# A decoder layer on eight cores: norm statistics in column halves, three chunks at a time; attention in 26 steps; 16-column back products; a last feed-forward group in parts

## What is computed

```python
h = x * (1 + sc1) + sh1                          # adaLN, from c
q, k, v, pool_in, ga, gb = split(h @ w_in)
# branch A: 3 groups (window, dilation) of 4 heads, banded 128-blocks, ALiBi, softmax;
#           the groups of a head slot are mixed by their softmax denominators
branch_a = att @ w_branch_att
# branch B: trailing means over 2/4/8/16 positions minus the token, per-group linear map
branch_b = (pooled @ w_pool_group * pool_scale) @ w_branch_pool
mixer_out = (sigmoid(ga) * branch_a + sigmoid(gb) * branch_b) @ w_out
x = layer_norm(alpha * x + g1 * mixer_out)
h2 = x * (1 + sc2) + sh2
ffn = (silu(h2 @ w_gate) * (h2 @ w_up)) @ w_down
x = layer_norm(alpha * x + g2 * ffn)             # D_MODEL 1024, SEQ 2048, D_FF 2816
```

## Time and profile before

| what | value |
|---|---|
| time, median of 3 runs | 2016.94 us (2016.87 to 2017.34) |
| the profiled execution | 2017.5 us, span of the slowest core 2016.1 us |
| span of the eight cores | 2013.8 to 2016.1 us, mean granted TensorE clock 0.995 |
| TensorE busy | 1941.8 us, 96% of the span |
| VectorE, ScalarE, GpSimd busy | 891.0, 781.1, 139.8 us |
| TensorE in the chain that ended last | 95% |

### The profile page before, as it was taken

How to read it: one execution, slowest core, us unless ns; L and a number is a source line. 1 busy time by engine, 2 the same in 40 slices (tenths; PEclk the granted TensorE clock), 3 DMA queues, 4 the chain that set the end, 5 groups by cost and what they waited for, 6 DMA issues and landing times.

```text
span 2016.1 us, 33562 instructions; the slowest of 8 cores (2013.8 to 2016.1 us)
## 1 busy us (share of the span) xinstructions
PE 1941.8 (96%) x11808; PEld 998.1 (50%) x11808; DVE 891.0 (44%) x1417; ACT 781.1 (39%) x1343; POOL 139.8 (7%) x268
## 2 busy tenths in 40 slices
PE   1999999999999999999999999999999999999995
PEld 0566654444446544444455566444444664444442
DVE  0446643552326435525265664354232553552326
ACT  0555532641026326410266553255101632651026
POOL 1110100000000000100000000000000000000000
PEclk9999999999999999999999999999999999999998
DMA  9965843444345635557451125344444473444432
GB/s 193 229 96 101 149 123 63 74 79 78 67 81 126 157 63 115 84 115 158 73 121 38 33 54 133 68 74 64 74 83 77 102 189 64 74 71 72 77 64 84
DMA packets 58962, 193.49 MB, mean 96 GB/s; under 512 B 6832, under 2 KB 6832, under 8 KB 57520
## 3 DMA queue, kind: packets, MB, share of 16 engines
q0 software_dynamic: 38016, 136.20, 40.7%
q1 hardware_dynamic: 20784, 55.14, 8.5%
HBM read 300.24 MB, written 18.87 MB: 158 GB/s over the span
## 4 chain that ended last, share of the span: by engine, by line
PE 95%; DMA 2%; DVE 1%; ACT 1%; issue 1%; POOL 0%; DVEq 0%; ACTq 0%; SPq 0%; POOLq 0%
PE ps L372 84%; PE ps L1024 4%; PE ps L805 3%; PE ps L621 2%; PE ps L594 1%; DMA T<-xT 1%; DMA wring<-w_ada 1%; DVE T L832 1%; DVE T L838 0%; PE ps L415 0%; DVE T L939 0%; ACT sg_t L985 0%; ACT u_t L507 0%; ACT hT L468 0%; POOL wring L189 0%
## 5 line engine op out<-in xcount | busy, mean ns | idle before, releaser
L372 PE MATMUL ps<-T,wring 128*128 128x512 bf16 x4864 | 1078.5, 379 | 4.2 <-ACT sg_t L985 4.2
L372 PEld LDWEIGHTS ps<-T,wring 128*128 128x128 bf16 x4864 | 475.7, 98 | 578.9 <-issue 6.7
L372 PE MATMUL ps<-hT,wring 128*128 128x512 bf16 x1792 | 413.9, 381 | 13.8 <-ACT hT L468 13.4
L985 ACT ACTIVATE sg_t<-ps 128x512 f32<-128x512 f32 x176 | 103.2, 596 | 553.3 <-PE ps L372 546.5
L986 DVE TENSOR_TENSOR T<-ps,sg_t 128x512 bf16<-128x512 f32 x176 | 120.2, 691 | 421.1 <-PE ps L372 379.7
L939 DVE SCALAR_TENSOR_TENSOR T<-ps,GA,T 128x512 f32<-128x512 f32 x256 | 192.1, 750 | 208.5 <-PE ps L372 206.4
L372 PEld LDWEIGHTS ps<-hT,wring 128*128 128x128 bf16 x1792 | 170.0, 98 | 219.2 <-issue 26.8
L372 PE MATMUL ps<-wring,hT 128*128 128x256 bf16 x1856 | 214.3, 273 | 2.1 <-ACT u_t L507 1.7
L372 PEld LDWEIGHTS ps<-wring,hT 128*128 128x128 bf16 x1856 | 184.3, 107 | 23.8 <-issue 2.9
L608 DVE TENSOR_TENSOR T<-ps,bias_t 128x256 f32<-128x256 f32 (+1 forms) x232 | 107.0, 499 | 61.7 <-PE ps L594 47.1
L613 ACT ACTIVATE T<-T 128x256 bf16<-128x256 f32 (+1 forms) x232 | 104.0, 478 | 69.8 <-DVE T L608 63.1
(11 more groups left out here) (80 smaller groups left out, 1072.0 us busy)
## 6 DMA issues: line engine op xcount, KB each, us to landing
wring<-w_gate POOLq DMA_DIRECT2D x44, 512.0 KB, 6.6
wring<-w_up POOLq DMA_DIRECT2D x44, 512.0 KB, 7.0
T<-xT SPq DMA_DIRECT2D x32, 512.0 KB, 9.5
wring<-w_down POOLq DMA_DIRECT2D x32, 512.0 KB, 7.2
outT<-T SPq DMA_DIRECT2D x64, 256.0 KB, 4.3
T<-xT SPq DMA_DIRECT2D x14, 1024.0 KB, 11.3
wring<-w_ada POOLq DMA_DIRECT2D x24, 512.0 KB, 8.8
wring<-w_pi POOLq DMA_DIRECT2D x16, 512.0 KB, 6.2
```

What stands on the lines that cost most here:

```text
L372: fns = [lambda lhsT=lhsT, rhs=rhs, i=i: nc.tensor.matmul(psum[bank][:, cols[0]:cols[1]], lhsT, rhs, start=(i == 0), stop=(i == n - 1)) fo ...
L985: k.op(ACT, lambda: nc.scalar.activation(sg_t[:, si, :], psum[bg][:, :], AF.Silu), reads=[ps_reg[bg]], writes=[r_sg[si]])
```

## The change

1. **Norm statistics.** The stationary matrix is now 128x64. The product with the copy goes to partitions 0 to 63 and that with the square to partitions 64 to 127 of one held bank, by the left and the right column half of the array. They are issued for three chunks in one group, when four chunks are fed: with chunk n fed, chunks n-3 to n-1. The staging has six buffers (three more lie in `t12_t`). Mean and mean square now stand on half of the partitions each, so `ln_moments` has three ScalarE operations in place of two and `ln_rstd` three in place of two.
2. **Attention.** `att_all` replaces the six phases by 26 steps over all of them. A step issues the outs of two block pairs (those scored two steps earlier), the scores of two block pairs, and then the other units, with the bias and exp operations between them. There are eight softmax buffers for each head of the pair instead of six. Units of the pooling branch (`pj[2]`, `bd[1]`, `pj[3]`) that stood behind attention are spread over the last six steps.
3. **Bands.** The back product has 16 columns instead of 128, and a unit is one group.
4. **The end.** In the last half of the last sequence the weights of the last gate and up products are loaded into `hT`, which is free by then, and the group is computed by token half: gate, up and down products of tt=0; gate and up of tt=1 with the norm passes of tt=0 between them; and down products of tt=1 in two quarters of 256 columns, each with its own statistics and norm.
5. Norm passes of the second norm are split in two background steps each.

```diff
--- before
+++ after
-LAG = 2
-NPT = 6
+NPT = 8
...
-        def att_phase(ph, fill, vroll):
-            scores, out = att_parts(ph)
-            n = 8 + LAG
-            share = spread(fill, n)
-            for i in range(n):
-                if i < 8:
-                    scores(i)
-                for f in share[i]:
-                    f()
-                if i >= LAG:
-                    o = i - LAG
-                    out(o)
-                    if o >= 1 and vroll:
-                        vroll[o - 1]()
-            if vroll:
-                vroll[7]()
+        def att_all(fills):
+            parts = [att_parts(ph) for ph in range(6)]
+            vnext = {ph: v_units(ph // 2 + 1, ACT) for ph in (1, 3)}
+            for t in range(26):
+                fill = list(fills[t])
+                if t >= 2:
+                    po, so = divmod(t - 2, 4)
+                    for pr in (2 * so, 2 * so + 1):
+                        parts[po][1](pr)
+                    if po in vnext:
+                        ready = 8 if so == 3 else 2 * so + 1
+                        vu = vnext[po]
+                        fill += vu[:ready - (8 - len(vu))]
+                        del vu[:ready - (8 - len(vu))]
+                post = []
+                if t < 24:
+                    ph, sp = divmod(t, 4)
+                    for pr in (2 * sp, 2 * sp + 1):
+                        post += parts[ph][0](pr)
+                n = max(len(fill), 1)
+                for i in range(max(n, len(post))):
+                    if i < len(post):
+                        post[i]()
+                    if i < len(fill):
+                        fill[i]()
...
+                            opening = hf == 0 and tau == 1
+                            mm(s_ * 128, 128, tau, 2 if opening else 0, True, opening)
+                            if not opening:
+                                mm(s_ * 128, 16, tau - 1, 1, False, True)
...
-            i0 = 2 * (feed["n"] % 3)
...
+            i0 = feed["n"] % 6
             feed["n"] += 1
-            k.op(ACT, lambda: nc.scalar.copy(ybs_t[:, i0, :], ysrc), reads=yreg, writes=[r_ybs[i0]])
-            k.op(ACT, lambda: nc.scalar.activation(ybs_t[:, i0 + 1, :], ysrc, AF.Square), reads=yreg, writes=[r_ybs[i0 + 1]])
-            feed["q"].append((key, m, i0))
-            while len(feed["q"]) > 2:
-                stats_pe()
-
-        def stats_pe():
-            key, m, i0 = feed["q"].pop(0)
-            if m == 0:
-                stat[key] = (new_bank(hold=True), new_bank(hold=True))
-            for j in range(2):
-                bk = stat[key][j]
-                k.group([lambda bk=bk, j=j: nc.tensor.matmul(psum[bk][:, :], onesm[:], ybs_t[:, i0 + j, :], start=(m == 0), stop=(m == KC - 1))],
-                        reads=[r_ybs[i0 + j], r_ones], writes=[ps_reg[bk]])
+            k.op(ACT, lambda: nc.scalar.copy(stat_buf(i0, 0, w), ysrc), reads=yreg, writes=stat_regs(i0))
+            k.op(ACT, lambda: nc.scalar.activation(stat_buf(i0, 1, w), ysrc, AF.Square), reads=yreg, writes=stat_regs(i0))
+            feed["q"].append((key, m, i0, w))
+            if len(feed["q"]) > 3:
+                stats_pe(3)
...
+        def stats_pe(n):
+            fns, rds, wrs = [], [r_ones], []
+            for _ in range(n):
+                key, m, i0, w = feed["q"].pop(0)
+                if m == 0:
+                    stat[key] = new_bank(hold=True)
+                bk = stat[key]
+                for j in range(2):
+                    fns.append(lambda bk=bk, j=j, m=m, i0=i0, w=w: nc.tensor.matmul(
+                        psum[bk][64 * j:64 * j + 64, 0:w], onesm[:, 0:64], stat_buf(i0, j, w), start=(m == 0), stop=(m == KC - 1)))
+                rds += stat_regs(i0)
+                wrs.append(ps_reg[bk])
+            k.group(fns, reads=rds, writes=wrs)
...
+        def ln_moments(key, si, w=512):
+            bk = stat[key]
+            s1 = 2 + 2 * si
+            mean = psum[bk][0:64, 0:w]
+            k.op(ACT, lambda: nc.scalar.activation(st_t[64:128, 0, 0:w], mean, AF.Square), reads=[ps_reg[bk]], writes=[r_st[0]])
+            k.op(ACT, lambda: nc.scalar.copy(st_t[0:64, s1, 0:w], mean), reads=[ps_reg[bk]], writes=[r_st[s1]])
+            k.op(ACT, lambda: nc.scalar.copy(st_t[64:128, s1, 0:w], mean), reads=[ps_reg[bk]], writes=[r_st[s1]])
+
+        def ln_rstd(key, si, w=512):
+            bk = stat[key]
+            s0 = 1 + 2 * si
+            var = st_t[64:128, 0, 0:w]
+            k.op(DVE, lambda: nc.vector.tensor_tensor(var, psum[bk][64:128, 0:w], var, ALU.subtract),
+                 reads=[ps_reg[bk], r_st[0]], writes=[r_st[0]])
...
+            for p0 in (0, 64):
+                k.op(ACT, lambda p0=p0: nc.scalar.activation(st_t[p0:p0 + 64, s0, 0:w], var, AF.Exp, scale=-0.5), reads=[r_st[0]], writes=[r_st[s0]])
...
+        def closing_loads(f0):
+            def mk(q, src):
+                return lambda: k.dma(POOL, tl_h[q], [(hT[:, q, :].rearrange("p (k c) -> p k c", c=256), src)], writes=r_hT[q])
+            return [mk(q, src[f0 // 2 + i]) for i in range(4) for q, src in ((i, w_gate), (4 + i, w_up))]
...
+            run([f1_unit(b, f0, fl, 0, st) for fl in range(nf)], bg, 1)
+            while bg:
+                bg.pop(0)()
+            for m in range(KC):
+                if m % 2 == 0:
+                    slots[m // 2] = wload(down_load(f0, f1, m // 2))
+                f2_unit(b, nf, m, 0, slots, False)()
+                stats_feed((b, 2, 0), m, 0, 512)
+            units = [f1_unit(b, f0, fl, 1, st) for fl in range(nf)]
+            units[0]()
+            stats_flush()
+            ln_moments((b, 2, 0), 0)
+            units[1]()
+            ln_rstd((b, 2, 0), 0)
+            bg = ln2_steps(b, t0, 0, 512, 0)
+            run(units[2:], bg, 2)
+            for q in range(2):
+                c0 = 512 + 256 * q
+                for m in range(KC):
+                    f2_unit(b, nf, m, c0, slots, False, 256)()
+                    stats_feed((b, 2, 1 + q), m, c0, 256)
+                    if q == 0:
+                        if bg:
+                            bg.pop(0)()
+                    else:
+                        if m == 1:
+                            ln_moments((b, 2, 1), 1, 256)
+                        elif m == 2:
+                            ln_rstd((b, 2, 1), 1, 256)
+                            bg = ln2_steps(b, t0, 512, 256, 1)
+                        elif m > 2:
+                            bg.pop(0)()
+                            bg.pop(0)()
+            stats_flush()
+            ln_moments((b, 2, 2), 0, 256)
+            ln_rstd((b, 2, 2), 0, 256)
+            return bg + ln2_steps(b, t0, 768, 256, 0)
...
+            last = spread(pj[0] + pj[1] + bd[0] + pj[2] + bd[1] + pj[3], 6)
+            for i in range(4):
+                last[2 + i] = last[2 + i] + nu[2 * i:2 * i + 2]
+            att_all(fills + last)
...
-            run(pj[2] + bd[1] + pj[3] + bd[2] + bd[3], bg, 1)
+            run(bd[2] + bd[3], bg, 1)
```

213 lines of the change are left out of this document (107 added, 106 removed).

## The result

| kernel | time, median | ratio to before |
|---|---|---|
| before | 2017.1 us | 1 |
| after | 2060.1 us (2060.44 and 2059.68) | 1.0213, 95% interval 1.0191 to 1.0235 |

The change makes the kernel 2.1% slower (1.9 to 2.4%). In two of the four runs of after (2352.7 and 2420.7 us) one die ran at a lower granted clock, 0.81 to 0.85 against 0.985 of the other die; they are left out. The forecast was 2022 us with a range to 2036: the sign was right, and the time lies 24 us above the range and 38 us above the forecast. All comparisons with before that follow are ratios on the same chip; the median of before was 2017 to 2023 us on the chips used.

What follows compares the result with a forecast made beforehand. TensorE, busy 96% of the span, was taken as the bound; -17.3 + 3.5 - 7.2 - 2.4 + 30.4 - 2.0 = +5.0 us on the median of 2016.94 gives 2022 us. Own range 2013 to 2031, full range 2006 to 2036.

Steps and rivals of the forecast that it cites:

- The clock rival: TensorE's clock falls in each of seven 3.6 us statistics waits: +18 us, 2040 us; chance 0.10.
- n = 12 waits: Statistics group at n = 12 waits for chunk 11's square behind ScalarE's moments and 1/sigma: 3.6 us a norm.
- Statistics: Norm statistics in column halves, one unit behind: waits of 7.1 us a norm outweigh saved products, +30.4 us for seven norms.
- the rival of 2048 us: Column halves of the statistics products do not run together at 512 columns: +26 us, 2048 us; chance 0.03.
- form changes: Switches of the TensorE array's form between neighbouring matmuls, in attention and statistics: 0.10 us each.
- Attention: New attention order has 148 changes of array form instead of 321: -17.3 us, with new waits counted against it.
- +3.5 us of waits: New TensorE waits in attention, at t=23's scores (2.4 us for two sequences) and phase boundaries (about 1.1); bounds 0 and 6.
- Bands: In the band units, 240 back products of 16 columns save 0.030 us each: -7.2 us, bounds 0 and -7.7.
- The part -2.4 for u_t: Pooling units' waits for u_t go because the norm's VectorE passes are spread over twice the units: -2.4 us.
- The end: Last group by token half with a half-size closing chain: 111.8 against 113.8 us, -2.0 us, bounds -6 and +3.
- The sum: All terms over the whole kernel: +5.0 us, giving 2022 us; chance of the forecast 0.45.

Runs made afterwards that it cites:

- fill mixed: Changed kernel with statistics and end of before, and projection and band units of the last six attention steps reordered; ratio to before 0.9900, 2003 us.

## Why the prediction was wrong, point by point

**The clock rival had the right size and the wrong chance.** This is the step that failed: the sum put the clock behind the new waits at nothing, and it is 23 of the 38 us by which the forecast was missed. The rival asked for 2.6 us behind each of seven 3.6-us waits, +18 us, and got a chance of 0.10 with the reason that the trace of before has no wait of such a length behind the start. But the earlier trace rows were a case of exactly this mechanism, with nothing that speaks against it at 3.6 us (the windows of the profile print a clock of 1.00 there only because the trace has no clock record ahead of 53.80 us; half speed from 48.51 to 53.80 is a loss of 2.6 us, the figure that the rows give); the forecast itself created seven waits in which it could act, and then left the price out of the sum. In the profile of after the seven n = 12 waits carry 30.7 us of half clock, 13.9 us of time; filling them gave back 12.3 us. So even the rival's +18 was somewhat high for these seven; attention (5.5 us) and the closing group (3.8) make it 23 us. What the Trainium skill says in "TensorE: Matmul & The Clock Gate", Part 1, that an idle stretch puts the clock back to its lower level, agrees with these rows. What no row of before could tell is that the clock would also fall behind the attention waits of 1.2 and 2.0 us, whose ends are 2.4 us apart.

**Statistics: right.** Forecast +30.4 for seven norms without the clock, thus 34.7 for eight. The kernel with the statistics alone has eight: +53 us, less 17 us of clock, is +36. The waits were forecast as 0.85, 0.85, 0.85, 3.6 and 1.0, and are 0.77, 0.77, 0.70, 3.81 and 0.70 to 1.08. The n = 12 chain came out as counted: moments, cast, square, table load, exp, exp, cast and square of chunk 11 in a row on ScalarE.

```profile
379.61 0.59 ACT L853 ACTIVATE st_t<-ps 64x512 f32<-64x512 f32 x1
...
382.92 1.28 ACT L863 ACT_TABLE_LOAD   x1
...
385.02 1.34 ACT L866 ACTIVATE st_t<-st_t 64x512 f32<-64x512 f32 x2
386.39 0.62 ACT L825 CAST t_t<-T 128x512 bf16<-128x512 f32 x1
387.10 0.63 ACT L826 ACTIVATE t_t<-T 128x512 bf16<-128x512 f32 x1
```

Square now starts 0.71 behind cast instead of 0.52; that both write one buffer with one entry in the register of hazards, so that the second waits for the first, is the reading of the code and was not tried. It is small beside the rest. Column halves at 512 columns do run together, six in 0.77 us: the rival of 2048 us did not come. The rule of the Trainium skill beside it ("TensorE: Matmul & The Clock Gate", Part 3, The mechanism: a weight load overlaps only across row groups) does not hold for these groups by the same 0.77 us. A group without a wait adds 0.875 - 0.648 = 0.23 us of form changes where I had 0.20. A misreading without effect on the sum: the largest waits of before behind the start are not those for u_t but four of up to 1.0 us for L985, 4.2 us in all.

**Attention: the saving right, the waits too small.** -17.5 against -17.3 for the forms. This is the second term that was mis-sized: the sum had +3.5 us of waits in all, and in the two attention stretches of after TensorE waits 8.2 and 4.8 us, where before it waited 0 and 0.8, so +12.2. The place was named (t = 22, its scores at t = 23) and priced 1.2 us per sequence; there it is 4.4 us, since L739 waits for L656 twice, the out products wait for the adds 1.22 and the scores 2.01; and each time the clock falls. Attention was to be some 14 us shorter in two sequences, and the two stretches are 3.0 us shorter. The working set VectorE's work of the step (5.9 us) against TensorE's (3.6) and took the lag at one point only, the scores. In after it shows at four points that add up, 0.37 + 0.77 + 1.22 + 2.01 = 4.4 us.

**Bands: products right, the sum too good.** 0.025 us per short product against 0.026. The bands alone gave 4.5 us of the 7.2, because 2.0 us of new waits for u_t stand against them. The part -2.4 for u_t was laid to the norm passes, and in the kernels that have them about 1 us of these waits is left.

**The end: -2.0 forecast, +3.0 measured** against the end of before, with old statistics; in after it is +8.4 us. I had put 1.2 us in front of each of the two changes from gate and up to down; the first is 1.2, the second 5.25. The cause is seen in the timeline of VectorE and ScalarE there:

```profile
1990.37 0.69 DVE L1026 TENSOR_TENSOR T<-ps,sg_t 128x512 bf16<-128x512 f32 x1 [3.42 <-PE ps L377]
...
1995.33 1.28 ACT L1025 ACT_TABLE_LOAD   x1
...
1997.33 0.69 DVE L1026 TENSOR_TENSOR T<-ps,sg_t 128x512 bf16<-128x512 f32 x1 [5.54 <-ACT sg_t L1025]
...
2008.06 0.69 DVE L1026 TENSOR_TENSOR T<-ps,sg_t 128x512 bf16<-128x512 f32 x1 [1.49 <-ACT sg_t L1025]
...
2010.24 0.81 ACT L913 ACTIVATE T<-T,prm 128x512 f32<-128x512 f32 x1 [2.29 <-DVE T L878]
2010.96 0.58 ACT L1025 ACTIVATE sg_t<-ps 128x512 f32<-128x512 f32 x1
2011.64 0.69 DVE L1026 TENSOR_TENSOR T<-ps,sg_t 128x512 bf16<-128x512 f32 x1 [1.49 <-ACT sg_t L1025]
```

A unit needs 3.46 us on TensorE. Between the products L1026 of the second and the third unit pass 1997.33 - 1990.37 = 6.96 us, because 1/sigma with its two exp passes and two table loads stands on ScalarE ahead of the silu: 3.5 us behind. The lag is never made up, because each later unit takes 2011.64 - 2008.06 = 3.58 us in a ring (product, center, scale, norm pass, silu, product), 0.12 us more than TensorE needs, and the down products meet the whole of it. Two norm steps per unit closed a ring over two engines; the sums per engine that I looked at have slack.

**The sum.** The parts timed alone add up to +53 - 4.5 + 1.4 + 3.0 = +53 us, with the end read from the stages; after has +43. Some 6 us of the difference are the shorter stages of 277 us, which no kernel with one part has (280.5 and 279.8 with the bands alone) and which are likely due to the split norm passes. The rest is about as large as the uncertainties together; that part of it is the eighth norm, which the closing group runs in other pieces, is likely and not shown.

## What to carry to other kernels

A wait on TensorE is not priced by its length alone: where a change puts a wait like those here (3.8 us, or 1.2 and 2.0 us in close order) into a stream that was full, add 1.7 to 3.0 us for the clock behind it, as a part of the forecast and not as a rival. Before units are moved, add up for each step not the work of each engine but the ring of who waits for whom; short units that free TensorE quickly need long ones between them. A saving on TensorE that is paid by giving a statistics chain one unit less lead is worth less than it looks: here 2.2 us a norm saved could not be kept at either distance.

The parts that pay are the short back products and the 26-step attention with its fill mixed; with the old statistics, and with the norm passes split as in the change, they make a kernel of 0.990 of before. The waits of 0.7 to 0.8 us at n = 3, 6 and 9, and the two of up to 1.6 us that the mixed fill left, had no half clock behind them.

## What was not expected of the hardware

Unread products made the kernel 12.3 us faster, by nothing but the clock. The granted clock fell for 3.41 us at some waits of 3.8 us and for 6.83 us at others of the same length in the same kernel (five and three of the eight with the statistics alone); at the n = 12 waits of 512 columns in the two traces, after and statistics alone, the five long stretches begin 0.8 to 1.7 us before the wait ends, and the ten short ones at its end or up to 1.5 us behind it. What sets the moment of the fall stays open.
